# The first mixer's gate multiplied into its output weights instead of into its products

## What is computed

```python
for l in range(DEPTH):                       # DEPTH = 2
    mod = (c_act @ w_ada[l] + b_ada[l])[:, None, :]
    shift_m, scale_m, gate_m, shift_f, scale_f, gate_f = jnp.split(mod, N_MOD, axis=-1)
    h = rms_norm(x, norm_mix[l]) * (1.0 + scale_m) + shift_m
    x = x + gate_m * hybrid_mixer(h, w_in[l], ..., w_out[l])   # ends in concat([out_a, out_b]) @ w_out
    h = rms_norm(x, norm_ffn[l]) * (1.0 + scale_f) + shift_f
    x = x + gate_f * hierarchical_moe(h, ...)
...
# out_b of hybrid_mixer, the gated linear attention (GLA) half:
out_b = merge_heads(rms_norm(o_b, gla_gain)) * jax.nn.silu(g_r)
```

## Time and profile before

| | us |
|---|---|
| median of three runs (1791.63 to 1795.76) | 1793.73 |
| the profiled execution | 1800.85 |
| its span from first to last instruction | 1798.7 |

### The profile page before, as it was taken

The page is one execution under the profiler, slowest core; times in us unless marked ns, Lnnn a source line. Parts: engine busy times, 40 slices in busy tenths (PEclk is TensorE's granted clock), DMA queues, the critical chain, the costliest instruction groups (busy, mean ns, idle before and its releaser), DMA issues.

```text
span 1798.7 us, 24694 instructions
## 1 busy us (share of the span) xinstructions
PE 1647.3 (92%) x10344; PEld 1412.5 (79%) x10344; DVE 1179.5 (66%) x1311; ACT 924.9 (51%) x1128; POOL 101.3 (6%) x68
## 2 busy tenths in 40 slices
PE   5999868999998999679999998998999999979998
PEld 2577548999987677568888897786899987869996
DVE  1544565999998645757888898666555576745554
ACT  1443136777776453346766676445444443544442
POOL 0010000011010110000101011000000011000000
PEclk8899878999999999879999999989999999989999
DMA  9766252999998766319998996252465541515551
GB/s 346 257 234 219 109 210 99 376 346 364 357 346 293 253 215 234 116 41 325 334 332 328 340 354 215 55 187 74 142 196 192 183 120 34 201 48 193 193 194 65
DMA packets 132243, 392.08 MB, mean 218 GB/s; under 512 B 23200, under 2 KB 36384, under 8 KB 107552
## 3 DMA queue, kind: packets, MB, share of 16 engines
q1 hardware_dynamic: 125008, 386.11, 60.0%
q10 hardware_dynamic: 7120, 4.33, 1.2%
HBM read 389.37 MB, written 1.05 MB: 217 GB/s over the span
## 4 chain that ended last, share of the span: by engine, by line
PE 73%; DVE 11%; DMA 8%; ACT 6%; POOL 1%; issue 1%; SPq 0%; DVEq 0%; ACTq 0%; POOLq 0%
PE ps L1113 13%; PE ps L459 11%; PE ps L2077 10%; PE ps L1127 6%; PE ps L439 6%; DVE spl L366 5%; PE ps L1577 5%; ACT spl L357 4%; DMA ring<-in_w_up 3%; PE ps L1601 2%; PE ps L501 2%; DMA ring<-in_w_ada 2%; PE ps L1553 2%; PE ps L518 1%; PE ps L1637 1%; PE ps L623 1%
## 5 line engine op out<-in xcount | busy, mean ns | idle before, releaser
L366 DVE TENSOR_TENSOR spl<-ring,spl 128x2048 fp32r<-128x2048 f32 (+2 forms) x318 | 730.5, 2299 | 275.5 <-ACT spl L357 274.1
L357 ACT ACTIVATE spl<-ring 128x2048 fp32r<-128x2048 f32 (+2 forms) x318 | 603.7, 1899 | 310.3 <-PE ps L459 108.0
L1113 PE MATMUL ps<-spl,ur 128*128 128x256 f32 x3072 | 375.2, 282 | 6.5 <-DVE spl L366 5.6
L1113 PEld LDWEIGHTS ps<-spl,ur 128*128 128x128 f32 x3072 | 363.9, 192 | 7.5 <-DVE spl L366 6.4
L459 PE MATMUL ps<-hh,spl 128*128 128x256 f32 x1728 | 207.9, 282 | 2.8 <-DVE hh L422 2.8
L459 PEld LDWEIGHTS ps<-hh,spl 128*128 128x128 f32 x1728 | 205.6, 190 | 5.7 <-issue 4.7
L1127 PE MATMUL ps<-spl,hh 128*128 128x512 f32 x768 | 186.8, 392 | 2.6 <-DVE hh L1298 2.0
L2077 PE MATMUL ps<-spl,ur 128*128 128x512 f32 x768 | 176.7, 389 | 0.0
L2077 PEld LDWEIGHTS ps<-spl,ur 128*128 128x128 f32 x768 | 143.2, 188 | 29.2
L1127 PEld LDWEIGHTS ps<-spl,hh 128*128 128x128 f32 x768 | 140.4, 188 | 30.6 <-issue 2.4
L439 PE MATMUL ps<-spl,hh 128*128 128x512 f32 x480 | 130.5, 426 | 0.1
(11 more groups left out here) (353 smaller groups left out, 1744.0 us busy)
## 6 DMA issues: line engine op xcount, KB each, us to landing
ring<-in_w_up SPq DMA_DIRECT2D x96, 1024.0 KB, 5.6
ring<-in_w_down SPq DMA_DIRECT2D x96, 1024.0 KB, 5.5
ring<-in_w_gate SPq DMA_DIRECT2D x64, 1024.0 KB, 5.4
ring<-in_w_ada SPq DMA_DIRECT2D x48, 1024.0 KB, 7.5
ring<-in_w_in SPq DMA_DIRECT2D x34, 1024.0 KB, 6.5
ring<-in_w_out SPq DMA_DIRECT2D x16, 1024.0 KB, 7.8
ring<-in_w_in SPq DMA_DIRECT2D x8, 384.0 KB, 3.4
gate<-in_b_ada ACTq DMA_DIRECT2D x4, 512.0 KB, 5.9
```

Of the source, the lines that this page charges most:

```text
L357: sc.activation(t.hi, t.raw, ACT.Copy).then_inc(s_hi, 1)
L366: v.tensor_tensor(t.lo, t.raw, t.hi, ALU.subtract).then_inc(s_lo, 1)
L1113: ins = pe.matmul(ps[:, 2 + q, 256 * z:256 * z + 256], le, ri, start=(k == 0 and j == 0 and z == 0), stop=(k == 7 and j == 2), skip_group_ ...
```

## The change

`dve_gate_out` (new) takes the place of the multiply in `dve_add`. DVE multiplies a landed out tile in place in the ring by `gate`, its 1024 values repeated for the tile's two rows of weights (128 x 2048 elements). ACT's high part of an out tile now waits for that multiply instead of for the tile's DMA. The four products are added to `x` straight from PSUM. `dve_split1` fixes where the multiplies stand in DVE's lane 0: that of out0 just before its low part's turn, and those of out1 to out3 each one step before the low part of the tile ahead of it.

```diff
+                if t in out_tiles:
+                    sc.wait_ge(s_og, out_tiles.index(t) + 1)
+                else:
+                    sc.wait_ge(s_w[t.slot], t.landed)
...
-        def dve_add(v, c, i, p, gated):
+        def dve_add(v, c, i, p):
             xs = x[:, i, c * 512:(c + 1) * 512]
-            if gated is None:
-                v.tensor_tensor(xs, xs, p, ALU.add).then_inc(s_x, 1)
-            else:
-                tmp = xn[:, i, c * 512:(c + 1) * 512]
-                v.wait_ge(*own_dve(v.tensor_tensor(tmp, p, gate[:, gated, c * 512:(c + 1) * 512], ALU.mult)))
-                v.tensor_tensor(xs, xs, tmp, ALU.add).then_inc(s_x, 1)
+            v.tensor_tensor(xs, xs, p, ALU.add).then_inc(s_x, 1)
...
+        def dve_gate_out(v, l, t):
+
+            w = T["out", l, t]
+            v.wait_ge(s_w[w.slot], w.landed)
+            if t == 0:
+                v.wait_ge(s_adf, ada_n[l, 5] + 1)
+            raw = w.raw.rearrange("p (a b) -> p a b", b=1024)
+            v.tensor_tensor(raw, raw, bc(gate[:, 0, :], 1, 2), ALU.mult).then_inc(s_og, 1)
+
+        def dve_split1(v, l):
+            first = T["out", l, 0].m
+            while dve_at.m <= T["up", l, 0].m:
+                if dve_at.m == first:
+                    dve_gate_out(v, l, 0)
+                    yield
+                if 0 < dve_at.m + 1 - first < 4:
+                    dve_gate_out(v, l, dve_at.m + 1 - first)
+                    yield
+                dve_lo(v, T["up", l, 0])
+                yield
```

More of the change, by code:

```diff
@@ L21 @@
 OUT2 = (1, 0, 2, 3)
-ORDER = {("mix1", 0, "PE"): "454005050555050665050555050665012350123125530123501213213255101250255045045045054554504504504500040455050000", ("mix1", 0, "ACT"): "004445066505066505123016201235312312132123510120625456050500644450000", ("mix1", 0, "DVE"): "00446506506666506506666152300123152312123015604254645404504464044054450000",
[1 row of a table removed]
+ORDER = {("mix1", 0, "PE"): "454005050555050665050555050665012350123125530123501213213255101250255045045045054554504504504504045505000000", ("mix1", 0, "ACT"): "004445066505066505123016201235312312132123510120625456050506404450000", ("mix1", 0, "DVE"): "004465065066665065066661523001231523121230156042546454045044604044054450000000",
[1 row of a table added]
          ("mix2", 0, "PE"): "40000404000012300120123014230104123412020413041231232112042303043043012301321241230310123124210123023400", ("mix2", 0, "ACT"): "40055005012301204314215423152413210412302043035031241203431210424131223044", ("mix2", 0, "DVE"): "4005540405012312350125011242435131241235241312412304123052045305433401213234120412133210412341232123044", ("mix2", 0, "POOL"): "",
@@ L307, in program @@
         s_sq, s_ms, s_rs, s_xn = sem("squares"), sem("mean_squares"), sem("row_rstd"), sem("rows_normed")
-        s_staged = sem("mix1_staged")
+        s_staged, s_og = sem("mix1_staged"), sem("out_tile_gated")
         s_xT, s_st, s_hT = sem("transposed"), sem("stage_scaled"), sem("stage_split")
@@ L344, in program @@
         splits = [t for t in loads if t.m is not None]
+        out_tiles = [T["out", l, t] for l in range(2) for t in range(4)]
         act_at, dve_at = Mem(), Mem()
@@ L353, in act_hi @@
                 act_at.m += 1
-                sc.wait_ge(s_w[t.slot], t.landed)
+                if t in out_tiles:
+                    sc.wait_ge(s_og, out_tiles.index(t) + 1)
+                else:
+                    sc.wait_ge(s_w[t.slot], t.landed)
                 if t.m >= SPLIT:
@@ L864, in dve_mix1 @@
                 v.tensor_tensor(hT[1][:, ks, :], m1.stage[:, ks, :], hT[0][:, ks, :], ALU.subtract).then_inc(s_hT, 1)
-            steps(ORDER["mix1", l, "DVE"], dve_split(v, T["up", l, 0]), *(dve_heads(v, l, lane) for lane in range(3)), dve_gla(v, l),
+            steps(ORDER["mix1", l, "DVE"], dve_split1(v, l), *(dve_heads(v, l, lane) for lane in range(3)), dve_gla(v, l),
                   dve_ada_lane(v, l), dve_main1(v, g, l))
@@ L872, in dve_mix1 @@
                         v.wait_ge(s_used, T["out", l, 3].m + 1)
-                    dve_add(v, c, i, ps[:, out_banks[2 * i + c], :], 0)
+                    dve_add(v, c, i, ps[:, out_banks[2 * i + c], :])
         def dve_main1(v, g, l):
@@ L2031, in dve_mix2 @@
                         v.wait_ge(s_used, T["out2", l, 3].m + 1)
-                    dve_add(v, c, i, ps[:, OB[2 * c + i], :], None)
+                    dve_add(v, c, i, ps[:, OB[2 * c + i], :])
         def pool_mix2(po, g, l):
```

## The result

The changed kernel takes 1797.63 us in the median of 20 runs (1792.04 to 1811.43), the kernel of before 1792.68 us in 20 runs beside them (1786.65 to 1799.51). The ratio is 1.0037 with a 95% interval of 1.0020 to 1.0055. The change makes the kernel slower, by 3.6 to 9.9 us.

The account below looks back on a forecast made before the run. It took PE, busy 92%, to bound the kernel as a whole, with the tails hanging on out2's matmuls. Layer 0's plus 4.4 and layer 1's plus 4.0 made plus 8.4 on 1793.73: 1802.1 us, range 1797 to 1806.

Parts of the forecast that it names:

- (2): Rival: PE keeps its clock over layer 0's gap at 230.6, giving plus 4.6 us, 1798.3; chance 7%.
- (3): Rival: layer 1's delay is given back in the experts' waits for weights, leaving layer 0's 4.4, 1798.1; chance 9%.
- The tail hangs on up0's low part: Both layers' tails: up0's low part stands ahead of the additions and needs out2's place, so out2's matmuls set the end.
- The additions, minus 2.5 a layer: Each layer's tail: adds step at about 0.61, ACT's squares set the pace, 3.63 us instead of 6.15.
- Layer 0, 1.5 us later and 24 matmuls more: PE's out block behind the modulation step: plus 1.5 and 5.4 us, less 2.5 in the tail, plus 4.4.
- Layer 1, the second copy: DVE's second copy of the GLA output comes behind added multiplies and low parts, plus 3.3 to 3.7 us, taken as 3.5.
- PE's wait ahead of L702: Layer 1: PE waits for DVE's later state step, plus 0.9 us.
- the two low parts stand ahead of L1009: Layer 1: out3's and gate0's low parts delay PE's second transposes 2.3 us more; out2's start moves by 5.8.
- The clock: Layer 1: longer PE gaps slow out2's 24 matmuls, plus 0.7 us, between nothing and 1.4; layer 0 keeps its slow start.
- (1): Rival: the gain alone counts, the moved work lying in unwaited time, 5.0 us off, 1788.7; chance 6%.
- The sign that I named for it: Sign against the forecast: the mixture of experts takes several microseconds less than now.

Follow-up runs that it names:

- e5: The kernel of before with up0's low part moved behind the four additions, the gate still multiplied into the products; ratio 0.9966 to the kernel of before.
- e6: The changed kernel with e4's orders in both layers and up0's low part moved behind the additions; ratio 0.9956 to the kernel of before.
- e1: The changed kernel's instruction orders with the arithmetic of before, so no multiply in the ring; ratio 1.0032 to the kernel of before.
- e2: The changed kernel with layer 0 reordered: PE's order of before, out0's low part earlier, out1's behind the GLA chain; layer 0 38.06 us, ratio 1.0006 to before.
- e3: The changed kernel with layer 1's second copy ahead of out2's low part and one low part ahead of each L1009 pair; layer 1 63.25 us, ratio 1.0008 to before.
- e7: The kernel of before with four delay instructions of 128 x 2048 on DVE ahead of each layer's additions; ratio 1.0117 to the kernel of before.
- e4: The changed kernel with the reorderings of e2 and e3, and layer 0's second 12 out1 matmuls behind the modulation step; ratio 0.9972 to the kernel of before.

## Why the prediction was right

It said 1802.1 us, plus 8.4 on 1793.73. The ratio gives plus 6.6, the two medians plus 4.95 and the stretches plus 5.2. The direction, the mechanism and the places were right, the size was some 2 to 3 us too large. The measured median, 1797.63, lies 4.5 below the forecast and only 0.6 above the lower end of the range, and it is nearer to rivals (2) and (3), 1798.3 and 1798.1, which the range took in. So the time alone does not confirm the working, and that it fell inside the range has some luck in it. What confirms the working is the traces and the experiments. By its steps:

**The tail hangs on up0's low part.** Right, and shown by e5, which moves that instruction alone.

**The additions, minus 2.5 a layer.** Measured from the first addition to the last square: 251.02 - 247.74 = 3.28 and 758.41 - 755.13 = 3.28, where 3.63 was expected and 6.15 stood before, so minus 2.9. The adds step at 0.62 (2.48 for four) as taken. The squares step at 0.62 and not at the 0.73 I read from the last one of the chain, which holds the wait for its second instruction. The new add that reads PSUM costs what the old add from SBUF did. That such an add is not in the trace of before was wrong: L473 is one, in the second mixer, and its eight instances there take 0.69 us each. It would have given the price without a bound. The 62 cycles by which the Trainium skill ("VectorE: DVE Perf Modes", TRN2 errata) puts a PSUM source above an SBUF source are not seen here: the new L476 takes 0.70 in e6's chain, L477 took 0.69 before.

**Layer 0, 1.5 us later and 24 matmuls more.** The block starts after 4.99 us of idle PE, 230.22 - 210.41 = 19.81 us into the stretch, before 18.31: plus 1.50, as worked out. The second 24 end at 243.39, 32.98 into it, before 26.85: plus 6.1 where 6.9 was expected. The missing 0.8 is the first 24, which took 7.7 and not 8.5 us. The 72 took 248.81 - 230.22 = 18.6, not 19.4. e1 and e2 show that the order is the cause.

**Layer 1, the second copy.** Expected plus 3.3 to 3.7, measured 32.75 - 29.51 = plus 3.2. PE's wait ahead of L702 was put at 0.9 and is 0.89. (The start of L703 before is 719.35. The 719.51 of the working is the end of the matmuls ahead of it.) That the two low parts stand ahead of L1009 brings the second transposes to plus 5.4 (743.21 - 690.85 against 744.08 - 697.16), expected 5.8. e3 shows both parts.

**The clock.** This is the term of the sum that was mis-sized. I took plus 0.7 for layer 1, since PE's gaps grow, with nothing and 1.4 as ends. The sign was wrong: out2's 24 took 6.56 us where before they took 7.15, so minus 0.6. With layer 0's 0.8 that is 2.1 of the 3.2 us by which my sum exceeds the stretches. The rest is 0.4 in each tail and 0.3 in layer 1's copy and low parts. The granted clock of the two blocks in the changed kernel:

```profile
225.30:230.20 4.90, 0.00 (x0) 0.00 (x0) 4.83 (x5) 1.91 (x1) 0.00 (x0) 0.74 0.70 293
230.20:237.90 7.70, 7.68 (x25) 6.22 (x26) 6.57 (x3) 1.91 (x1) 0.00 (x0) 0.72 0.64 230
237.90:248.90 11.00, 10.91 (x49) 8.70 (x47) 5.74 (x4) 4.27 (x3) 0.00 (x0) 1.00 0.63 228
```

In the first 7.7 us the mean is 0.72, which lies between the two levels (0.5 and 1.0): the clock rose inside this stretch. Before, it was 0.55 over 6.7 us. The sentence of the prediction that names the Trainium skill ("TensorE: Matmul & The Clock Gate", Part 1: the number of slow matmuls at a start differs from run to run) is not what these traces show in layer 0. Where two kernels have the same instructions in the same order there, their starts came out alike: the first 24 took 7.71 us in after and 7.79 in e3, the 48 took 13.96 before, 14.06 in e5 and 14.09 in e7. They differ between kernels whose instructions there differ. In layer 1 the spread between like kernels is larger, 12.92, 13.25 and 12.81 us for the 48 in before, e5 and e7.

**The rivals.** (1), the gain alone, is excluded as a description of this kernel by both stretches. e4 shows that it is a matter of order: 4.0 us can be had. (2), PE keeping its clock in layer 0, was wrong as stated, since the clock was low at the block's start, but the block was warm sooner: 0.8 of its 3.1 us came, and 0.6 more in layer 1. (3), a return of layer 1's delay by the experts, is excluded by e7, with room for 3 us. The sign that I named for it, experts that take several microseconds less, does stand in the trace of after: 439.8 us from the last square of layer 0 to layer 1's stretch, before 444.1. But e3, which has the same instructions as after up to there, has 444.2, so one trace can't carry this sign.

**What stayed open.** The span of after is 5.4 us shorter than that of before, though its two stretches are 5.2 longer. The other 10.6 us come from stretches that the change leaves alone: 5.3 ahead of layer 0's (210.41 against 215.75, and as much already at 151.25 against 156.58), 4.2 between the two and 1.1 behind them. In the traces of this study layer 0's stretch starts between 210.4 and 215.8, from the last square of layer 0 to layer 1's stretch it is 439.4 to 444.2 us, and behind layer 1's last square 1026.2 to 1038.0. These do not follow the size of the change: e1 (plus 6.7) has 443.6, e7 (plus 18.5) 442.0, before 444.1. Their cause stays open.

## What to carry to other kernels

A scale that is moved from the products into the weights takes work out of the tail, but puts it between a transfer and the first engine that reads the tile. It pays only if what it delays ahead of the tail is less than what it saves in it (in e4's layer 0, 2.2 against 2.9 us), and in the changed kernel the order alone cost 6.7 us where the tails saved 5.7. Before making a tail cheaper, look at what stands in front of it in the same queue: one low part that was not needed yet, moved behind four additions, gave 5 us without touching the arithmetic, and after it the gate in the ring gave nothing more that could be measured. And read a small effect from a stretch between two events around it, since the span of a single trace pointed the other way.

## What the runs showed of the hardware

In these traces a longer gap on PE did not make the start behind it slower. The same 48 matmuls of out2 and out3 took 13.96 us after 3.52 us of idle PE and 14.06 after 3.51 in e5, but 12.77 after 4.87 in e6 and 12.82 after 3.74 in e4. In e7 they took 14.09 after 3.42, and in e2 13.95 after the longest gap, 7.05:

```profile
232.18 12.77 PE L622 MATMUL ps<-spl,hh 128*128 128x512 f32 x48 [4.87 <-DVE spl L370]
...
232.10:238.80 6.70, 6.62 (x22) 5.32 (x23) 4.72 (x4) 3.72 (x2) 0.00 (x0) 0.75 0.52 179
```

The mean granted clock over the first 6.7 us was 0.75 there and 0.55 before. In e4 and e6 PE's last 12 matmuls with a `w_out` tile stand directly ahead of the gap; in before, e2, e5 and e7 the 2 us of small matmuls of the modulation step stand between. The six values fall into two groups by this, 13.95 to 14.09 and 12.77 to 12.82 us, so chance is an unlikely reason. But the small matmuls can't be the whole of it. They stand ahead of the gap in after and e3 too, where the first 24 took 7.71 and 7.79 us after 4.99 of idle PE, and in e1, 7.15 after 2.79, against 8.54 before. What sets the length of such a start stays open. The length of the gap alone does not.
